# Middle norm's mean square from three sums by blocks, and products that begin with two groups transposed

## What is computed

```python
x = first_block(...)                  # ends in a gated feed-forward product and rms_norm(x, final_norm_g)
# second_block
h = modulate(rms_norm_2(x, pre_norm_mix[l]), shift_m, scale_m)
... = jnp.split(h @ w_in[l], split_at, axis=-1)
...
o = jnp.concatenate([o_n, o_m], axis=-1) @ w_o[l]
x = x + gate_m[:, None, :] * rms_norm_2(o, post_norm_mix[l])
h = modulate(rms_norm_2(x, pre_norm_ffn[l]), shift_f, scale_f)
f = jnp.square(jax.nn.relu(h @ w_up[l])) @ w_down[l]
x = x + gate_f[:, None, :] * rms_norm_2(f, post_norm_ffn[l])
```

## Time and profile before

| | us |
|---|---|
| median of 3 runs | 2790.65 (2789.14 to 2790.76) |
| profiled execution, device time | 2791.04 |
| its span | 2789.2 |
| PE, DVE, ACT, POOL busy | 2725.9, 1771.2, 1323.8, 169.5 |
| mean granted clock of PE, of full speed | 0.993 |

### The profile page before, as it was taken

One profiled execution on the slowest core, in us unless ns is written; L12 is line 12 of the kernel. 1 busy time (PEld: TensorE's weight loads), 2 busy tenths in 40 slices (PEclk: granted clock), 3 DMA queues, 4 the chain that ended last, 5 costly groups with the idle time before them and its releaser, 6 DMA issues.

```text
span 2789.2 us, 34781 instructions
## 1 busy us (share of the span) xinstructions
PE 2725.9 (98%) x13302; PEld 2328.2 (83%) x13302; DVE 1771.2 (64%) x2022; ACT 1323.8 (47%) x1678; POOL 169.5 (6%) x132
## 2 busy tenths in 40 slices
PE   8999999999999999999999999998989999999998
PEld 8999988888888888888888799887868888888886
DVE  4477488776578888765555564547775756645455
ACT  5555444454445454434454444346455344354443
POOL 0001620000000000000000002620000000000000
PEclk9999999999999999999999999999999999999999
DMA  8554068887477777775556556640756867755653
GB/s 284 164 170 131 1 242 275 292 277 262 161 262 273 274 276 275 271 252 189 188 181 208 172 198 197 199 148 1 271 174 203 276 206 241 257 182 180 196 181 121
DMA packets 293266, 579.60 MB, mean 208 GB/s; under 512 B 9168, under 2 KB 46192, under 8 KB 292112
## 3 DMA queue, kind: packets, MB, share of 16 engines
q1 hardware_dynamic: 291296, 566.08, 60.2%
q0 software_dynamic: 1120, 8.57, 0.8%
q10 hardware_dynamic: 720, 3.15, 0.3%
HBM read 575.66 MB, written 2.10 MB: 207 GB/s over the span
## 4 chain that ended last, share of the span: by engine, by line
PE 95%; DVE 3%; ACT 1%; issue 1%; DMA 0%; SPq 0%; POOL 0%; DVEq 0%; ACTq 0%
PE GP L984 29%; PE GP L986 29%; PE GP L985 28%; PE TA L959 2%; PE TB L959 2%; PE TB L607 1%; PE TB L426 1%; PE GP L401 0%; PE TA L1353 0%; DVE wlo L1937 0%; DVE x L2379 0%; PE GP L1194 0%; PE TA L1194 0%; PE GP L1181 0%; DMA x<-in_x 0%
## 5 line engine op out<-in xcount | busy, mean ns | idle before, releaser
L1937 DVE TENSOR_TENSOR wlo<-raw,whi 128x1024 fp32r<-128x1024 f32 (+2 forms) x904 | 1088.2, 1217 | 812.2 <-ACT whi L1446 803.3
L1446 ACT CAST whi<-raw 128x1024 fp32r<-128x1024 f32 (+2 forms) x904 | 923.6, 1029 | 1170.9 <-PE GP L986 1108.6
L984 PE MATMUL GP<-whi,hhi 128*128 128x512 f32 (+2 forms) x1792 | 689.2, 385 | 1.9 <-issue 1.4
L986 PE MATMUL GP<-whi,hlo 128*128 128x512 f32 (+2 forms) x1792 | 681.0, 380 | 0.0
L985 PE MATMUL GP<-wlo,hhi 128*128 128x512 f32 (+2 forms) x1792 | 680.2, 380 | 0.0
L984 PEld LDWEIGHTS GP<-whi,hhi 128*128 128x128 f32 x1792 | 337.9, 189 | 52.6 <-issue 3.2
L986 PEld LDWEIGHTS GP<-whi,hlo 128*128 128x128 f32 x1792 | 337.6, 188 | 52.5
L985 PEld LDWEIGHTS GP<-wlo,hhi 128*128 128x128 f32 x1792 | 338.1, 189 | 50.5 <-issue 1.0
L984 PE MATMUL GP<-whi,bhi 128*128 128x512 f32 x704 | 276.7, 393 | 0.2 <-DVE blo L1998 0.2
L1925 DVE SCALAR_TENSOR_TENSOR ada_acc<-raw,csig,ada_acc 128x512 f32<-128x512 f32 x360 | 270.2, 751 | 10.2
L986 PE MATMUL GP<-whi,blo 128*128 128x512 f32 x704 | 274.3, 390 | 0.0
(11 more groups left out here) (428 smaller groups left out, 2555.2 us busy)
## 6 DMA issues: line engine op xcount, KB each, us to landing
raw<-in_w_up SPq DMA_DIRECT2D x108, 1024.0 KB, 5.3
raw<-in_w_down SPq DMA_DIRECT2D x108, 1024.0 KB, 5.1
raw<-in_w_ada SPq DMA_DIRECT2D x96, 1024.0 KB, 5.2
raw<-in_w_gate SPq DMA_DIRECT2D x44, 1024.0 KB, 5.3
raw<-in_w_in SPq DMA_DIRECT2D x48, 856.0 KB, 4.7
raw<-in_w_xkv SPq DMA_DIRECT2D x32, 1024.0 KB, 5.7
raw<-in_w_in SPq DMA_DIRECT2D x24, 1024.0 KB, 5.0
raw<-in_w_in SPq DMA_DIRECT2D x24, 864.0 KB, 4.7
```

The source lines that it names most:

```text
L984: pe.matmul(o, ahi[:, kt, t], whi[r][:, k, 0:q.width], start=first, stop=False)
L986: m = pe.matmul(o, alo[:, kt, t], whi[r][:, k, 0:q.width], start=False, stop=last)
L1446: nc.scalar.copy(whi[(2 * g + s) % NRING][:, :, 0:q.width], raw[j % NSLOT][:, 2 * s:2 * s + 2, 0:q.width])\
L1937: TTo(wlo[r][:, :, 0:q.width], raw[j % NSLOT][:, 2 * s:2 * s + 2, 0:q.width], whi[r][:, :, 0:q.width].bitcast(F32), ALU.subtract).then_inc ...
```

## The change

**The mean square of the middle norm.** The new x is x + ors * g, with g the gated block. Its mean square is xx + ors * (2xg) + ors^2 * gg, three sums. All three are taken by blocks while `w_oa` and `w_ob` run: ACT takes the squares of the old x (`x_squares`, behind units 8 to 10 of `w_oa` and 5 of `w_ob`) and of g (`gated_squares`), DVE the cross sums (`crossed`, behind each gated block). Behind the end of `w_ob` DVE does the last block's share, joins the sums with `ors` in four small steps and bounds the result from below by 1e-6.

**The additions.** Only the two pieces of block 0 are added ahead of the middle norm's first transposes. The other six stand in `mixed_pair`, between a group's full and its lower. Block 0 is scaled half by ACT and half by DVE.

**The products.** In both norms PE transposes groups 0 and 1 ahead of the product, and two groups each behind halves 0, 2 and 4 (`second_turns`). ACT's scalings and casts and DVE's fulls and lowers are put in the matching order, and the split of a weight unit stands between every two pairs. Both additions of `final_x` now stand behind unit 5 of `w_in2a`.

```diff
+                            if s == 0 and isinstance(it, int) and (it, b, u, "half") in points:
+                                points[it, b, u, "half"]()
...
+            def second_turns(i):
+                return {(0, 0, u, "half"): lambda u=u: (second_turn(i, 2 * u + 2), second_turn(i, 2 * u + 3)) for u in range(3)}
...
+            for g in range(2):
                 second_turn(0, g)
...
+                    points=second_turns(0))
...
-            for g in range(6):
+            for g in range(2):
...
             def second_scaled(i, k):
                 X, xn, r = seconds[i][0:3]
-                for h in range(NH):
+                if i:
+                    act.wait_ge(S("y_mix"), 2 * k + 2 if k else 1)
+                for h in range(NH if k else 1):
                     m = nc.scalar.activation(xn[:, h, 512 * k:512 * k + 512], X[:, h, 512 * k:512 * k + 512], ACT.Copy, scale=r[:, h:h + 1])
                 m.then_inc(S("p2_x"), 1)
...
-            def second_uppers(i):
-                second_scaled(i, 1)
-                second_scaled(i, 2)
-                for g in range(6):
-                    if g == 2 and i:
-                        split_hi(PH["up20"], 0, 1)
-                    if g == 4:
-                        second_scaled(i, 3)
-                    second_upper(i, g)
-
-            second_uppers(0)
-            phase(PH["w_in2a"], store(PH["w_in2a"], p2, lastcol=NSA_W - W2A), head={3: [lambda it: (second_upper(0, 6), second_upper(0, 7))],
+            second_scaled(0, 1)
+            second_upper(0, 0)
+            second_upper(0, 1)
+            second_scaled(0, 2)
+            second_upper(0, 2)
+            second_upper(0, 3)
+            second_scaled(0, 3)
+            phase(PH["w_in2a"], store(PH["w_in2a"], p2, lastcol=NSA_W - W2A), head={3: [lambda it: (second_upper(0, 4), second_upper(0, 5))],
...
+            def gated_squares(b, hs=range(NH)):
+                    act.wait_ge(S("og"), b + 1 if b < 3 else 4 + h)
+                    nc.scalar.activation(fbx[0], o2[:, h, 512 * b:512 * b + 512], ACT.Square, scale=D ** -0.5,
+                                         accum_out=xs[:, 16 + 4 * h + b:17 + 4 * h + b]).then_inc(S("gg_ss"), 1)
...
+                                     {8 + b: [lambda it, b=b: x_squares(b)] for b in range(3)},
...
-            phase(PH["w_ob"], joined(first_block, {3: [lambda it: post_block(0, 1)], 7: [lambda it: post_block(0, 2)],
-                                                   8: [lambda it: root_table()]}), lead=1)
+            phase(PH["w_ob"], joined(first_block, {3: [lambda it: post_block(0, 1)], 4: [lambda it: gated_squares(0)], 5: [lambda it: (x_squares(3), gated_squares(1))],
+                                                   7: [lambda it: post_block(0, 2)], 8: [lambda it: root_table()], 9: [lambda it: gated_squares(2)]}), lead=1)
...
-            for h in range(NH):
-                post_square(0, 3, h, GP[:, 2 + h, :])
+            for j, h in enumerate((1, 0)):
+                act.wait_ge(S("norm_ss"), 29 + j)
+                if j:
+                    act.wait_ge(S("og"), 4)
+                nc.scalar.activation(junk[0][:, :], GP[:, 2 + h, :], ACT.Square, accum_out=beta[:, 4 * h + 3:4 * h + 4]).then_inc(S("norm_ss"), 1)
+            gated_squares(3, (0,))
             post_root(0)
-            for i in range(7):
-                b, h = divmod(i, 2)
-                act.wait_ge(S("y_mix"), i + 1)
-                act.wait_ge(S("norm_ss"), 31 + i)
-                nc.scalar.activation(junk[0][:, :], x[:, h, 512 * b:512 * b + 512], ACT.Square,
-                                     accum_out=beta[:, 8 + 4 * h + b:9 + 4 * h + b]).then_inc(S("norm_ss"), 1)
+            gated_squares(3, (1,))
...
-            second_uppers(1)
+            second_scaled(1, 0)
+            second_upper(1, 0)
+            second_upper(1, 1)
+            second_scaled(1, 1)
+            split_hi(PH["up20"], 0, 1)
+            second_upper(1, 2)
+            second_upper(1, 3)
+            second_scaled(1, 2)
...
+                phase(PH[f"up2{s}"], hooks, head={3: []} if s else {3: [lambda it: (second_upper(1, 4), second_upper(1, 5), second_scaled(1, 3))],
+                                                                    4: [lambda it: (second_upper(1, 6), second_upper(1, 7))]})
...
             def second_scale(i):
                 X, xn, r = seconds[i][0:3]
-                for h in range(NH):
+                for h in range(i, NH):
                     m = nc.vector.tensor_scalar(xn[:, h, 0:512], X[:, h, 0:512], r[:, h:h + 1], None, ALU.mult)
                 m.then_inc(S("p2_x0"), 1)
...
-            phase(PH["w_in2a"], {}, head={3: [lambda it: second_pair(0, 6)], 4: [lambda it: final_x(0)], 5: [lambda it: final_x(1)]})
+            phase(PH["w_in2a"], {}, head={3: [lambda it: second_pair(0, 4)], 4: [lambda it: second_pair(0, 6)],
+                                          5: [lambda it: (final_x(0), final_x(1))]})
...
+            def crossed(b, h):
+                link(nc.vector.scalar_tensor_tensor(junk[1][:, :], o2[:, h, 512 * b:512 * b + 512], 2.0 / D, x[:, h, 512 * b:512 * b + 512],
+                                                    ALU.mult, ALU.mult, accum_out=xs[:, 8 + 4 * h + b:9 + 4 * h + b]))
...
             def last_columns(it):
                 dve.wait_ge(S("mm_done"), block_end(PH["w_ob"], 0, 1) + NRING)
+                TTo(o2[:, 0, c3], GP[:, 2, :], gpb[0][:, c3], ALU.mult).then_inc(S("og"), 1)
                 dve.wait_ge(S("norm_ss"), 30)
-                TTo(o2[:, 0, c3], GP[:, 2, :], gpb[0][:, c3], ALU.mult)
-                post_mean(0)
-                TTo(o2[:, 1, c3], GP[:, 3, :], gpb[0][:, c3], ALU.mult).then_inc(S("evac1"), 1)
-
-            phase(PH["w_ob"], {4: [lambda it: gated(0, 1)], 8: [lambda it: gated(0, 2)], 10: [last_columns]}, lead=1)
-            dve.wait_ge(S("evac1"), 1 + PH["w_ob"].ev1)
+
+            phase(PH["w_ob"], {4: [lambda it: gated_sums(1)], 7: [x_means], 8: [lambda it: gated_sums(2)], 10: [last_columns]}, lead=1)
+            post_mean(0)
+            dve.wait_ge(S("og"), 5)
+            dve.sem_inc(S("evac1"), 1)
+            crossed(3, 0)
+            crossed(3, 1)
             post_scale(0)
-            for b in range(4):
-                for h in range(NH):
-                    post_add(0, b, h, "y_mix")
-            dve.wait_ge(S("y_mix"), 8)
-            link(nc.vector.scalar_tensor_tensor(junk[1][:, :], x[:, 1, c3], 1.0, x[:, 1, c3], ALU.mult, ALU.mult, accum_out=beta[:, 15:16]))
             modulation(1, 48, 5)
-            dve.wait_ge(S("norm_ss"), 38)
-            link(nc.vector.tensor_reduce(xsum, beta[:, 8:16].rearrange("p (a b) -> p a b", b=4), AX.X, ALU.add))
-            nc.vector.tensor_scalar(xmean, xsum, 1.0 / D, EPS, ALU.mult, ALU.add).then_inc(S("norm_ms"), 1)
+            dve.wait_ge(S("gg_ss"), 8)
+            link(nc.vector.tensor_reduce(xt[:, 2:6], xs[:, 8:24].rearrange("p (a b) -> p a b", b=4), AX.X, ALU.add))
+            nc.vector.tensor_scalar(xt[:, 6:7], xt[:, 4:5], ors[:, 0:1], xt[:, 2:3], ALU.mult, ALU.add)
+            link(nc.vector.tensor_scalar(xt[:, 7:8], xt[:, 5:6], ors[:, 1:2], xt[:, 3:4], ALU.mult, ALU.add))
+            nc.vector.tensor_scalar(xt[:, 8:9], xt[:, 6:7], ors[:, 0:1], xt[:, 0:1], ALU.mult, ALU.add)
+            link(nc.vector.tensor_scalar(xt[:, 9:10], xt[:, 7:8], ors[:, 1:2], xt[:, 1:2], ALU.mult, ALU.add))
+            nc.vector.tensor_scalar(xmean, xt[:, 8:10], EPS, None, ALU.max).then_inc(S("norm_ms"), 1)
+            post_add(0, 0, 0, "y_mix")
             dve.wait_ge(S("norm_rt"), 7)
             nc.vector.reciprocal(xrs, xroot).then_inc(S("raw_rs"), 1)
+            post_add(0, 0, 1, "y_mix")
             dve.wait_ge(S("raw_rs"), 7)
+            dve.wait_ge(S("y_mix"), 2)
             second_scale(1)
-            second_pair(1, 0)
+
+            def mixed_pair(b):
+                for h in range(NH):
+                    second_full(1, 2 * b - 2 + h)
+                    post_add(0, b, h, "y_mix")
+                    second_lower(1, 2 * b - 2 + h)
+
+            mixed_pair(1)
             split_lo(PH["up20"], 0, 1)
-            second_pair(1, 2)
-            second_pair(1, 4)
+            mixed_pair(2)
...
+                phase(PH[f"up2{s}"], hooks, head={3: []} if s else {3: [lambda it: mixed_pair(3)], 4: [lambda it: second_pair(1, 6)]})
```

More of the change, by code:

```diff
@@ L2379, in post_add, with gated_sums, x_means @@
                 nc.vector.scalar_tensor_tensor(x[:, h, c], osq[n][:, h, c], ors[:, h:h + 1], x[:, h, c], ALU.mult, ALU.add).then_inc(S(done), 1)
-            phase(PH["w_oa"], {3 + i: [lambda it, i=i: gate_column(0, 32, i)] for i in range(4)} | {8: [lambda it: gated(0, 0)]}, links=2)
+            def crossed(b, h):
+                link(nc.vector.scalar_tensor_tensor(junk[1][:, :], o2[:, h, 512 * b:512 * b + 512], 2.0 / D, x[:, h, 512 * b:512 * b + 512],
```

(11 more changed lines are left out.)

30 lines of the change are left out of this document (20 added, 10 removed).

## The result

| | before | after |
|---|---|---|
| median of 12 runs each, us | 2790.78 (2789.14 to 2793.65) | 2797.48 (2795.54 to 2800.86) |
| profiled execution: device time, span | 2791.04, 2789.2 | 2797.52, 2795.7 |

The ratio is 1.0025, with a 95% interval of 1.0017 to 1.0032: slower, clear of the noise, by a quarter of a per cent. The forecast was 2796.9.

What follows compares the result with a forecast made beforehand. TensorE was taken to hold 95% of the chain that ended last, with VectorE's chain ending the middle norm. Middle norm +3.1 and final norm +3.1 gave +6.2, a median of 2796.9 us, range 2794.0 to 2799.6.

Steps and rivals of the forecast that it cites:

- The first transpose: Middle norm: first transpose 7.5 us behind the end of `w_ob`, at 2048.5, which is 4.1 earlier.
- the sign of being wrong: Middle norm: the prediction is wrong if the first transpose comes at 2050 or later.
- `w_oa` and `w_ob` unchanged: The sums' work moved into `w_oa` and `w_ob` costs nothing; VectorE's free time before 2040.9 shrinks from 2.0 to 0.4.
- VectorE's round: Middle norm behind the first transpose: two groups and a weight unit's split take 8.68 us, three rounds 26.0.
- Ninth half: Middle norm: the ninth half, first of `up20`'s next block, begins at 2083.7 against 2080.63, +3.1.
- Low clock hidden in the middle norm: Middle norm: 1.8 us lost to low clock at the product's start stays inside slack; transposes at 2056.6, VectorE asks at 2058.3.
- The final norm: Final norm: -0.8 + 1.9 + 1.1 + 0.2 - 1.0 + 1.8 = +3.2, group by group +3.1, which was taken.
- +0.8 left: Final norm: the lower bound, what remains of the loss if the clock costs nothing.
- 3.2 to 4.0 us of steady work from there: Final norm: work needed from PE's restart at 1608.3 before full clock; 3.6 us at 1.2 GHz cost 1.8.
- The transposes count as work: PE's clock: the row of 2052.50, 3.2 us of transposes alone, has the product behind it begin at full clock.
- The sum: Both norms: +3.1 and +3.1 give +6.2, 2797.2 for a profiled run and 2796.9 for the median.
- the fall as a case of its own: Middle norm: the clock falls in PE's new 2.3 us gaps, +1.8, 2798.7, a second place up to 2799.6; chance 0.14.

Runs made afterwards that it cites:

- e10: The kernel before with the new order in the final norm alone, the middle norm as before; 2792.70 us, 0.9996 to 1.0014 of before.
- e6f: As e6, with seven unused transposes between the second turned group and the product of the middle norm; 2790.31 us, 0.9988 to 1.0006 of before.
- e2: The changed kernel with eight unused transposes between the final norm's second turned group and the product; 2795.90 us, 1.0007 to 1.0026 of before.
- e6: The changed kernel, middle norm: weight cast ahead of scaling, both fulls of a pair ahead of both lowers, adds kept; 2792.78 us.
- e3: The changed kernel with ScalarE's cast of each weight unit ahead of the scaling of x's next block in the middle norm; 2794.12 us.
- e1: The changed kernel with the final norm's interleave undone, the middle norm still changed; 2794.07 us, 1.0003 to 1.0021 of before.
- e11: The changed kernel with four unused transposes behind the final norm's second turned group; 2795.97 us, 1.0011 to 1.0029 of before.
- e4: The changed kernel without the six adds into x in the middle norm, order full, lower kept; output differs; 2796.89 us.
- e5: As e4, without the six adds, and with both fulls of a pair ahead of both lowers; output differs; 2792.57 us.
- e9: The changed kernel, final norm as before; middle norm: blocks 0 and 1 added early, four groups turned ahead, four unused transposes, pairs, cast first; 2788.55 us.
- e12: As e9, with the final norm's last two groups turned behind the third half of `w_in2a` instead of the second; 2784.89 us, 0.9981 of before.

## Why the prediction was right, by its steps

- **The first transpose**: forecast 7.5 us behind the end of `w_ob`, measured 7.93; gain 3.7 instead of 4.1. (It stands at 2052.11 only because `w_ob` ended at 2044.18 here; the sign of being wrong, 2050 or later, was set for an end at 2040.90.) The term that was short is the last one of small steps: the reduction, the four half-width steps and the maximum took 1.26 (2048.73 to 2049.99), where I had 0.85. The four are 0.27 each, where the small steps of the earlier trace rows stand 0.2 apart.
- **`w_oa` and `w_ob` unchanged**: right. 411.21 against 411.55 alone wouldn't show it, since this stretch moves by more; but e10, which has no sums there, took 409.00, and seven kernels with the sums took 408.95 to 409.04. VectorE's idle time at the end of `w_ob` is 0.42, forecast 0.4.
- **VectorE's round**: forecast 8.68, measured 8.56; the split behind the second lower's start 2.35 and 2.31. PE's waits were 1.75 and 1.89, forecast about 2.3: from the fifth to the seventh half PE was busy for 6.79 of 8.68 us, where the prediction's prices for two halves and two groups give 6.4 (2 x 2.73 + 0.93). Ninth half +3.1, forecast +3.1: the start was 0.4 dearer, three rounds 0.36 cheaper.
- **Low clock hidden in the middle norm**: right as to the time. VectorE's third full, at 2061.82 in after, waits for nothing, though the turned groups come only at 2060.81; filling was tried in e6f alone, where VectorE is no longer late, and gains 2.5 there. The size was off: the clock rose 4.8 us behind the product's start, where I had 3.2 to 4.0, and from the start of those transposes to VectorE's full it was 1.0 us, where I had 1.7.
- **The final norm**: forecast +3.1, usual +3.1, profiled +3.7. The start is 0.8 earlier, as forecast. e2, where the clock costs nothing, is 1.2 above before; the forecast's terms without the clock leave 1.4. (The wait before the fifth half is 0.55 to 0.76, where I had 1.1.) The prediction's lower bound, "+0.8 left", doesn't follow from its own terms. The clock is the other 1.9, forecast 1.8: "3.2 to 4.0 us of steady work from there" was 3.8 to 4.3 in six executions. Only in the profiled execution of after is this term too small: the rise came 5.9 us behind the restart (1607.49 to 1613.41) and cost 2.5. Why it came so late there stays open.
- **The transposes count as work**: the row of e2 shows the rise behind 3.0 us of nothing but transposes. The Trainium skill, page "TensorE: Matmul & The Clock Gate", section "Part 4: PE-mode transpose", says that the full clock doesn't engage for them; the row disagrees again.
- **The sum**: +6.2 forecast, +6.7 measured. The usual +3.1 and +3.1 give 6.2 in an execution that keeps its clock in the gap, and 7.8 in one that loses it; the median of 12 lies between them. The forecast had the fall as a case of its own, with 0.14, where it comes and goes between kernels that have the same middle norm. The mechanism and the sizes by stretches are borne out. That the total came within 0.6 us is partly luck, since unedited stretches move by 2 us and more.

## What to carry to other kernels

An earlier start is worth only what the chain behind it can keep: in the middle norm 3.7 us were won ahead of the first transpose and 6.9 lost behind it, because VectorE's steps were put in an order that made room for moved work and waited for casts (2.7 of it, e6), with a low clock at the product's start underneath (2.5 once VectorE kept up, e6f). Before instructions are moved in between two steps that hand work to and fro, count the round of the slowest engine, and put the piece that others wait for (the cast of the weights) ahead of the piece that is needed later (the scaling). And a TensorE that stops shortly ahead of a product can be kept at work with transposes that nobody uses: that was worth 1.9 and 2.5 us here.

## What the runs showed of the hardware

**The clock can't be forecast to the microsecond.** With the same activity ahead (1.54 and 1.56 us busy of 3.43 and 3.42), the granted clock stayed at 1.00 or fell to half, at 1.6 to 1.8 us a time. The rise isn't fixed either. Behind one and the same stop of 1.66 us ahead of `up20` it came 2.8 (e3), 3.3 (e2), 4.6 (e1), 4.8 (after), 6.1 (e11) and 6.2 us (e4) behind the restart.

**A stretch moves by microseconds without an edit.** From the ninth half of `w_in2a` to the end of `w_ob` the executions took 408.9 to 409.0 (eight of them), 410.2, 411.2 to 411.6 (three) or 416.1 us, though after, e2, e3, e4, e5, e6, e6f and e11 (408.9 to 411.6) have the same instructions there, and e9 and e12 too (411.25 and 408.96). The first stretch, up to the final norm, which is the same in all kernels, took 1601.9 to 1605.9. In the middle of the stretch between the norms lies attention, where PE has many short waits. 65 us of it in before, after, e2 and e1 (at the same times of the span; the work in them is about 4 us apart at most):

```profile
1880.00:1945.00 65.00, 53.17 (x359) 47.52 (x360) 47.78 (x115) 40.32 (x147) 0.00 (x0) 0.92 0.00 1
```

```profile
1880.00:1945.00 65.00, 51.12 (x353) 45.53 (x353) 48.79 (x120) 41.46 (x156) 0.00 (x0) 0.94 0.00 1
```

```profile
1880.00:1945.00 65.00, 52.27 (x377) 46.20 (x375) 46.98 (x113) 40.52 (x145) 0.00 (x0) 0.97 0.00 1
```

```profile
1880.00:1945.00 65.00, 54.67 (x335) 49.76 (x334) 45.37 (x111) 37.63 (x138) 0.00 (x0) 0.84 0.00 1
```

The mean clock is 0.97 in the execution of 409.0 us, 0.92 and 0.94 in those of 411, and 0.84 in that of 416. Cut by the work, 65 us from 250 us behind the ninth half of `w_in2a` on, all thirteen executions fall in line: 0.97 in the eight of 409, 0.95 in that of 410.2, 0.92 in the three of 411, 0.84 in that of 416. That the clock's spells make the difference fits all of them and was not tested by an edit. It bounds what a median can tell of this kernel: differences of 2 us between two kernels are better read from the cut stretches than from the total.
